# The first FFN's post-norm by halves of the tokens, from its last output blocks into the values' first group

## The reference

```
def rmsnorm(x, g):
    return x * rsqrt(mean(x * x, axis=-1) + EPS) * g

def swiglu(x, w_in, w_out):
    gate, up = split(x @ w_in, 2)          # D_FF = 2816
    return (silu(gate) * up) @ w_out

h = rmsnorm(x, ffn1_pre_norm)
x = x + 0.5 * rmsnorm(swiglu(h, w_ffn1_in, w_ffn1_out), ffn1_post_norm)
h = rmsnorm(x, mix_pre_norm)
z = h @ w_in       # queries, keys, values of 3 attention groups, and more
...
```

## Time and profile before

| | |
|---|---|
| median of 3 runs | 1489.06 us (1487.78 to 1489.80) |
| profiled execution | 1489.92 us, its span 1488.1 us |
| PE busy | 1477.8 us, 99% of the span |
| PEld busy | 1221.5 us, 82% |
| DVE busy | 722.7 us, 49% |
| ACT busy | 586.4 us, 39% |
| mean granted TensorE clock | 0.998 of 2.4 GHz |
| FFN output product on PE | about 248 to 367.7 us |
| values, group 0 on PE | 374.3 to about 396 us |

### The profile page before, as it was taken

One profiled execution on the slowest core, in us unless ns is written; L12 is line 12 of the kernel. 1 busy time (PEld: TensorE's weight loads), 2 busy tenths in 40 slices (PEclk: granted clock), 3 DMA queues, 4 the chain that ended last, 5 costly groups with the idle time before them and its releaser, 6 DMA issues.

```text
span 1488.1 us, 20133 instructions
## 1 busy us (share of the span) xinstructions
PE 1477.8 (99%) x7516; PEld 1221.5 (82%) x7516; DVE 722.7 (49%) x1153; ACT 586.4 (39%) x940; POOL 20.1 (1%) x35
## 2 busy tenths in 40 slices
PE   9999999999999999999999999999999999999998
PEld 7888888887898888888888888888878888888886
DVE  6444444223763455454246665654347444444223
ACT  5233233223432555553254654553344332233122
POOL 0000000000100000000000000000000000000000
PEclk9999999999999999999999999999999999999999
DMA  5322223332332222222322222223331222322332
GB/s 192 99 96 90 96 99 99 99 97 89 120 102 91 88 72 89 71 60 97 99 86 71 71 72 70 72 68 99 100 116 68 87 97 99 98 89 95 100 99 99
DMA packets 39397, 137.68 MB, mean 93 GB/s; under 512 B 4743, under 2 KB 4743, under 8 KB 39344
## 3 DMA queue, kind: packets, MB, share of 16 engines
q1 hardware_dynamic: 37728, 132.14, 27.4%
q0 software_dynamic: 1472, 4.76, 1.2%
q10 hardware_dynamic: 144, 0.04, 0.0%
HBM read 134.00 MB, written 2.13 MB: 91 GB/s over the span
## 4 chain that ended last, share of the span: by engine, by line
PE 96%; DVE 1%; ACT 1%; DMA 1%; issue 0%; SPq 0%; DVEq 0%; ACTq 0%
PE ps L290 27%; PE ps L291 27%; PE ps L292 27%; PE ps L872 1%; PE ps L874 1%; PE ps L873 1%; PE ps L1158 1%; PE ps L1138 1%; PE ps L1037 1%; PE ps L1038 1%; PE ps L1036 1%; PE ps L1518 1%; PE ps L1535 1%; PE ps L1123 1%; PE ps L1541 1%; PE ps L1505 1%
## 5 line engine op out<-in xcount | busy, mean ns | idle before, releaser
L269 ACT ACTIVATE whi<-raw 128x1024 fp32r<-128x1024 f32 x238 | 251.9, 1059 | 615.4 <-PE ps L292 553.9
L290 PE MATMUL ps<-hh,whi 128*128 128x512 f32 x1248 | 492.0, 394 | 1.8 <-DVE hl L748 1.0
L291 PE MATMUL ps<-hl,whi 128*128 128x512 f32 x1248 | 486.2, 390 | 0.0
L292 PE MATMUL ps<-hh,wlo 128*128 128x512 f32 x1248 | 485.9, 389 | 0.0
L274 DVE TENSOR_TENSOR wlo<-raw,whi 128x1024 fp32r<-128x1024 f32 x238 | 291.5, 1225 | 394.5 <-ACT whi L269 394.2
L290 PEld LDWEIGHTS ps<-hh,whi 128*128 128x128 f32 x1248 | 234.2, 188 | 55.8 <-issue 2.9
L292 PEld LDWEIGHTS ps<-hh,wlo 128*128 128x128 f32 x1248 | 234.3, 188 | 49.5
L291 PEld LDWEIGHTS ps<-hl,whi 128*128 128x128 f32 x1248 | 234.4, 188 | 46.9 <-issue 0.2
L451 DVE TENSOR_TENSOR tmp<-ps,rstd 128x512 f32<-128x512 f32 x44 | 30.4, 690 | 121.3 <-PE ps L292 121.3
L290 PE MATMUL ps<-whi,ah 128*128 128x512 f32 x176 | 68.5, 389 | 0.0
L292 PE MATMUL ps<-whi,al 128*128 128x512 f32 x176 | 68.5, 389 | 0.0
(11 more groups left out here) (269 smaller groups left out, 1748.3 us busy)
## 6 DMA issues: line engine op xcount, KB each, us to landing
raw<-in_wstream SPq DMA_DIRECT2D x242, 512.0 KB, 3.3
xt<-in_x_t SPq DMA_DIRECT2D x8, 256.0 KB, 5.7
out<-out_tok SPq DMA_DIRECT2D x8, 256.0 KB, 2.0
bias<-vec_dram POOLq DMA_DIRECT2D x8, 192.0 KB, 3.2
raw<-in_wstream SPq DMA_DIRECT2D x4, 256.0 KB, 4.7
bias<-vec_dram POOLq DMA_DIRECT2D x8, 128.0 KB, 3.3
v_mid<-v_tok POOLq DMA_DIRECT2D x2, 384.0 KB, 4.5
cst<-in_consts POOLq DMA_DIRECT2D x1, 640.0 KB, 5.8
```

Of the source, the lines that this page charges most:

```text
L269: nc.scalar.activation(whi[:, s, :], raw[:, s, :], ACT.Copy).then_inc(head_done, 1)
L290: nc.tensor.matmul(out, w, m, start=start, stop=False)
L291: nc.tensor.matmul(out, w, ml, start=False, stop=False)
L292: return nc.tensor.matmul(out, wl, m, start=False, stop=stop)
```

## The change

The last eight inner tiles (k = 14 to 21) of the last two output tiles (d = 6, 7) are computed apart, and by halves of the tokens: 256 columns first for both tiles, then the other 256. From there to the values' first group the norm runs by halves too.

- **PE**, `ffn1_out_pe`: blocks 0 to 19 hold the 132 products of d = 0 to 5 and 14 each of d = 6 and 7. Then blocks 22 (d = 6) and 23 (d = 7) are each gone through twice, for tokens 0 to 255 and for tokens 256 to 511, in banks 0 to 3: 96 matmuls of 256 columns in place of 48 of 512. The sum over the features is one matmul of 256 columns for each half, without the second one on `sq`; the first stands inside the second pass over block 22, the second in the values' first group before kt = 3.
- **PE**, `v_pe`: group 0 runs as token tiles 0 and 1 over all eight kt, then tiles 2 and 3. The bias vectors come after it. The twelve unread matmuls are gone.
- **Stream**: the values' blocks 0 and 1 come before the two last FFN blocks, as blocks 20 and 21, into buffers of their own (`whi_v`, `wlo_v`). Their heads and tails stand right behind those of block 19. Blocks 24 and 25 are the values' blocks 2 and 3.
- **ACT and DVE**, `ffn1_out_act`, `ffn1_out_dve`: the first 14 products of d = 6 and 7 are copied out as they are; DVE adds the second part to them (`joined`), ACT squares the sum, DVE adds the squares. Multiplication, addition, `hh` and `hl` are done for each d on 256 columns, all eight for the first half and then all eight for the second. The joins and additions of squares for the second half stand between the turns of the first. For d = 6 and 7 the gain is applied with `rstd` in one operation.
- The copies of value tiles 0 and 1 by ACT move in among the second half's `hh`. Some semaphore counts of the first norm are renumbered.

```diff
+        def ffn1_out_pe(pe):
+            first = FIRST["ffn1_out"]
...
+            for half in range(2):
+                for d in (KT - 2, KT - 1):
+                    if half == 0:
+                        pe.wait_ge(split_done, 2 * FIRST["v"] + d - 5)
+                    for i in range(KT):
+                        if half == 1 and d == KT - 2 and i == 4:
+                            pe.wait_ge(*counted("post1", "acc", KT - 1))
+                            nc.tensor.matmul(ps[:, 4, TOKENS[0]], ones[:], y0[:, TOKENS[0]], start=True, stop=True
+                                             ).then_inc(norm_sem("post1", "sum"), 1)
+                        k = SPLIT_K + i
+                        last = product(ps[:, out_bank(d, half), TOKENS[half]], *wcols(d % 2, i * P), ah[:, k, TOKENS[half]],
+                                       al[:, k, TOKENS[half]], i == 0, i == KT - 1)
+                    last.then_inc(block_done if half else sem("half_column"), 1)
...
+            square_half(6, 0)
+            square_half(7, 0)
+            post1_rstd_act(act, 0)
+            for d in range(3):
+                gained_half(d, 0)
+            square_half(6, 1)
+            gained_half(3, 0)
+            head(act, v, 0, 2 * v - 1)
+            gained_half(4, 0)
+            square_half(7, 1)
+            gained_half(5, 0)
+            post1_rstd_act(act, 1)
+            head(act, v, 1, 2 * v)
+            gained_half(6, 0)
+            gained_half(7, 0)
+            for d in range(KT):
+                gained_half(d, 1)
+                if d in (3, 5):
+                    v_leave_act(act, 0, d // 2 - 1)
...
+            joined(6, 0)
+            acc_half(6, 0)
+            joined(7, 0)
+            acc_half(7, 0)
+            for half in range(2):
+                for d in range(KT):
+                    scaled(d, half)
+                    if half == 0 and d == 2:
+                        joined(6, 1)
+                    elif half == 0 and d == 4:
+                        acc_half(6, 1)
+                        joined(7, 1)
+                    elif half == 0 and d == 5:
+                        acc_half(7, 1)
+                    if d >= 1:
+                        gained_half(d - 1, half)
+                    if half == 0 and d in (5, 7):
+                        tail(dve, v, d // 2 - 2)
+                    added(d, half)
+                gained_half(KT - 1, half)
...
+            for half in range(2):
+                for kt in range(KT):
+                    b, k = divmod(kt, 2)
+                    pe.wait_ge(*counted("pre2", "ready", KT * half + kt + 1))
+                    if half == 0 and kt == 3:
+                        pe.wait_ge(*counted("post1", "acc", KT + 1))
+                        nc.tensor.matmul(ps[:, 5, TOKENS[1]], ones[:], y0[:, TOKENS[1]], start=True, stop=True
+                                         ).then_inc(norm_sem("post1", "sum"), 1)
...
-            columns_pe(pe, "ffn1_out", "post1", FT, ah, al, sem("a_tail"), 1)
-            pe.wait_ge(*counted("post1", "left", KT - 1))
-            pe.wait_ge(*counted("post1", "last", 1))
-            bias_vectors_pe(pe)
-            pe.wait_ge(split_done, 2 * FIRST["v"] + 1)
-            for _ in range(12):
-                nc.tensor.matmul(ps[:, 1, :], whi[:, 0, 0:P], whi[:, 0, S:2 * S], start=True, stop=True)
+            ffn1_out_pe(pe)
```

## The result

| | before | changed kernel |
|---|---|---|
| median | 1488.73 us (1487.65 to 1490.46, 20 runs) | 1490.64 us (1489.70 to 1493.59, 20 runs) |
| ratio, 95% interval | | 1.0015, 1.0008 to 1.0022 |
| profiled execution | 1489.92 us, span 1488.1 | 1490.21 us, span 1488.4 |
| mean granted clock there | 0.998 | 1.000 |

The kernel became 1.9 us slower in the median, between 1.2 and 3.3 us by the interval of the ratio. That is 0.13% (0.15% by the ratio): clear of zero, within the 0.2% that counts as no change, and inside the range given. The forecast, 1492.1, was 1.5 us too high.

A forecast was written before the change was run, and what follows sets the result against it. PE bounds the kernel (96%), with DVE's queue to the v_tok copies ending within 0.2 us of it: 7.1 us more DVE work, started 4.1 earlier, gives 3.0 later, 1489.06 to 1492.1. Range, 8 in 10: 1487.8 to 1496.

The forecast's parts named there:

- What bounds it: PE's path and DVE's queue to the v_tok copies end within 0.2 us at group 1's third tile; the copies decide.
- PE's part: Last FFN blocks to group 1: 96 matmuls at 0.120; without waits third tile at 394.2, at most 3.7 us gained.
- rival of slow weight loads: Loads bound the 256-column matmuls: at 0.188, 4 us more, 1496; without overlap 1500; chance 0.05, of which 0.01 without overlap.
- The weight stream: Blocks 22 and 23 behind three splits: block 22 lands after 5.5 us, PE waits 1.0; with 3.3, waits 0.6 for block 23.
- rival of a late block 23: Block 23 lands 5.5 us after its issue, PE waits another 1.8: 1493.9; chance 0.09 together with the clock rival.
- When DVE starts: DVE begins the norm's elementwise work at 366.9 instead of 371.09, 4.1 us earlier.
- What DVE has to do: Norm to v_tok copies: 5.0 us for sixteen half turns at 1.39, 1.0 inserted work, 1.1 waiting for hh; 7.1 more.
- The sum: DVE's 7.1 us more work, started 4.1 earlier: v_tok copies end 3.0 us later, at 400.8.
- the list: PE's waits, second sum to group 1's third tile: 1.1, 1.6, 0.5, 2.1; with 1.0 and 0.35, 6.7 us against 3.7 gained.
- From the span to the time: The 3.0 us stay to the end: profiled 1489.92 becomes 1492.9, median of three runs 1489.06 becomes 1492.1.
- The clock rival: Fillers gone, PE idle 2.1 us behind bias vectors: a second clock fall costs 1.4 us, 1493.5; chance 0.09 with late block.
- The gain rival: Half turns of 1.08: copies end at 395.9, time 1487.1; inserted work hidden too, 1485.4; under 1486.1 had chance 0.07.

The follow-up runs named there:

- b_copies_first: Kernel before, with DVE's two v_tok copies and ACT's head moved ahead of the additions of squares 2 to 7; 1488.36 us, ratio 0.9997.
- b_no_fill: Kernel before without the twelve unread matmuls between the bias vectors and the values; 1490.33 us, ratio 1.0006.
- a_order1: Changed kernel with ACT's and DVE's queues reordered between the last FFN block and the bias copies, PE's queue and arithmetic kept; 1485.61 us, ratio 0.9976.
- b_half_turns: Kernel before with only the norm's turns cut into sixteen half turns of 256 columns; 1493.77 us, ratio 1.0033.
- a_copies_first: Changed kernel with DVE's two v_tok copies right behind the first tail, ahead of additions of squares, and ACT's head moved up; 1489.18 us, ratio 1.0003.
- a_both: Changed kernel with both edits: hl one turn later, and v_tok copies ahead of additions of squares; 1487.77 us, ratio 0.9989.
- a_order3: Changed kernel with another order of ACT's and DVE's queues: hl late, v_tok copies early, second head ahead of rstd; 1484.75 us, ratio 0.9975.
- a_fill_late: Changed kernel with seven unread matmuls in group 1 ahead of the third tile's wait for v_tok; 1491.29 us, ratio 1.0013.
- a_late_hl: Changed kernel with DVE making each hl one turn later; 1488.31 us, ratio 0.9998.
- a_fill: Changed kernel with the twelve unread 512-column matmuls put back ahead of the values' group 0; 1491.55 us, ratio 1.0016.
- a_order1_again: The kernel of a_order1 run once more, against the kernel before; 1484.83 us, ratio 0.9975.

## Why the prediction was right, point by point

- **What bounds it** (two chains 0.2 us apart, and the copies decide): right. b_copies_first confirms that only 0.3 us lay between them, and over all kernels of the table the lowest time follows the third tile within 1.1 us, from 2.3 us earlier to 5.1 later (b_no_fill aside, whose distance is of an execution with a fall).
- **PE's part** (96 matmuls at 0.120): right in the price of a matmul, short in the sum of the path. Timelines of PE and PEld:

```profile
356.80 0.28 PE L301 MATMUL ps<-al,whi 128*128 128x256 f32 x1
356.92 0.28 PE L302 MATMUL ps<-ah,wlo 128*128 128x256 f32 x1
```

```profile
356.80 0.19 PEld L302 LDWEIGHTS ps<-ah,wlo 128*128 128x128 f32 x1
356.92 0.19 PEld L300 LDWEIGHTS ps<-ah,whi 128*128 128x128 f32 x1
```

  Matmuls and loads stand 0.12 apart, with loads whose record is 0.19. By the rule of the Trainium skill (TensorE: Matmul & The Clock Gate, "What overlaps and what doesn't") and its figure for a load it would be 0.23, an estimate. The trace disagrees here too, and the rival of slow weight loads is out, with and without that rule. (Its price of 4 us was summed too low, too: 6.5 less 0.35 and 1.1 is 5.) The path as a whole was summed 1.4 us too short: 394.2 is 48.0 behind the head of block 19, and a_order1, where PE waits for nothing, takes 49.40. Group 0 with the sum inside it takes 22.7 there for the 22.2 put, the six matmuls of group 1 take 1.64 for 1.4. So the most that could be gained was 2.3 us and not 3.7.
- **The weight stream**: mis-sized. I took 5.5 us for block 22's load and a wait of 1.0; it was issued at 349.33, once block 20 was split, and its head ran at 353.80, some 4.5 us later, between the two rows that bounded it. So the other branch came, in which PE goes on at once and waits for block 23: 0.18 us, for 0.6 put. The rival of a late block 23 didn't come: its load was issued at 353.95, and its head ran at 357.17, 3.2 us later, without waiting for it:

```profile
353.80 1.06 ACT L273 ACTIVATE whi<-raw 128x1024 fp32r<-128x1024 f32 x1 [0.79 <-DMA raw<-in_wstream]
...
357.17 1.06 ACT L273 ACTIVATE whi<-raw 128x1024 fp32r<-128x1024 f32 x1
```

- **When DVE starts** (4.1 us earlier): 4.8 by the distance from the head of block 19, 24.89 before and 20.09 after. The 0.8 us less of waiting for the load is about the whole difference.
- **What DVE has to do** (7.1 us more): 7.6. The 5.0 for the halves measured 5.1, alone, in b_half_turns. The Trainium skill (VectorE: DVE Perf Modes, "The TRN2 errata") says that each operation pays a fixed cost and advises tiles of 512 elements or more. The trace agrees, in the single operation (0.69 for 512 columns, 0.42 for 256) and in turns where nobody waits (1.87 for 512 columns, twice 1.06 for 256). By these turns 2.0 us of the 5.1 are the fixed cost of DVE's own three operations. The rest is waiting, 0.34 us in each of sixteen half turns for 0.28 in each of eight whole ones, and that part the new orders take away. The 2.1 for inserted work and ACT measured 2.5; the largest piece of it is DVE's wait for ACT behind Ln, Exp and a head:

```profile
378.52 0.49 DVE L762 SCALAR_TENSOR_TENSOR hl<-xt,par,hh 128x256 fp32r<-128x256 f32 x1 [0.95 <-ACT hh L674]
...
381.06 0.48 DVE L762 SCALAR_TENSOR_TENSOR hl<-xt,par,hh 128x256 fp32r<-128x256 f32 x1 [0.58 <-ACT hh L674]
```

- **The sum** (3.0 us later): 2.8, from -4.8 and +7.6. Two mis-sized terms, 0.7 less and 0.5 more, nearly cancel, and that is luck. The waits on PE came where they were listed, each smaller: 0.77 for 1.1, 1.43 for 1.6, 0.15 for 0.5, 1.72 for 2.1. With the 0.18 for block 23 they make 4.3 for the 6.7 of the list. They are smaller since PE's own path is longer than I had it; the end is set by DVE's queue, so the 3.0 wasn't hurt.
- **From the span to the time**: this is the step that was furthest off. Of the 1.5 us that the forecast was too high, 0.3 are the median of before itself (1489.06 from three runs, 1488.73 from twenty), 0.2 the distance (3.0 for 2.8), and 0.9 that the medians differ by 1.9 and not by 2.8. The last isn't clear of noise, since the interval of 1.2 to 3.3 holds the 2.8. What fits it: the profiled execution of before had a clock fall of 1.4 us and a late load of some 1.0, and falls are more frequent in before. Of 33 runs of before in one comparison 19 had a mean clock of 0.998 or less, of the 20 of the changed kernel 7; at 1.4 us each this is an estimated 0.3 in the mean. The lowest times, mostly free of falls, still differ by 2.1, and the rest isn't explained. Nor was it found what sets the falls near 411 us. In the profiled executions before, a_copies_first, a_both, a_order1, a_order3, a_fill_late and b_no_fill show one between 408 and 420, each within 2 us of the end of the same spell of sums and one-column matmuls; the changed kernel, a_late_hl, a_fill, b_copies_first, b_half_turns and a_order1_again go through that spell without one, though the last is a_order1's very program.
- **The clock rival** (1.4 us by the new idle time): not in the profiled execution, and not shown for the others. The trace of a_fill has one fall 1.0 us behind that idle time; a_fill_late, which fills it, did not lower the median. That a fall can follow idle time of PE is seen in b_no_fill, and there it is dearer than put: 2.8 us, since the clock stays low for 6 us and not for 2.8.
- **The gain rival** (cheap half turns, 1487.1, and 1485.4 with everything hidden): wrong for this kernel, since the round trip through ACT held each turn at 1.40. With another order the kernel came to 1484.8 to 1485.6.

## What to carry to other kernels

When a chain of operations goes round over two engines, its pace is the round trip, not the sum of either engine's work: put the step that waits for the other engine a turn or two later before cutting the width, and cut the width only then. Count the price of the cut between turns without waits (here 2.12 us for 1.87), not against turns that hold a wait. Halving gained some 4 us in the median once the order of two queues was rewritten, 2.3 of them seen at group 1's third tile, and cost 1.9 us without that. Compare medians and lowest times, not two profiled executions: one granted-clock fall in one of them was worth half of the effect here, and one late load a third.

## What the runs showed of the hardware

- Without the twelve matmuls that nobody reads PE idles 2.8 us. In the trace of such a run the granted clock then stays at 0.50 for some 6 us, which costs 2.8, and six of eleven runs have a mean clock that fits this (b_no_fill).
- The fall comes in some executions of the same program and not in others (a_order1 and its repeat). An idle time of 1.7 us behind six matmuls of 512 columns was passed at 1.00 in the profiled execution of the changed kernel and followed by matmuls 0.43 apart in that of a_fill.
- A matmul of 256 columns costs 0.120 with a load of 0.19 for each; half of the 0.227 of 512 columns and 0.006 more. Halving the moving side cost PE 0.6 us in 96 matmuls.
- On DVE the three operations of a turn stand 1.87 us apart in sum on 512 columns and 1.06 on 256 where nobody waits (before, a_late_hl); with a round trip to ACT in the turn it is 2.15 and 1.40.
- The same load of 512 KB at the second FFN's output makes ACT wait from nothing (b_no_fill, a_late_hl) to 1.30 us (before), and PE's start behind it moves by 1.0 us.
